# Paged latent attention in a two-layer decoder step: score rows by sequence, token block and head, and value pages of 32 partitions

## The reference

```python
q_lat = jnp.einsum('bthd,rhd->bthr', q_nope, w_uk)
s_past = (jnp.einsum('bthr,bsr->bhts', q_lat, ckv_past)
          + jnp.einsum('bthd,bsd->bhts', q_rope, kr_past))
s_new = (jnp.einsum('bthr,bsr->bhts', q_lat, ckv_new)
         + jnp.einsum('bthd,bsd->bhts', q_rope, kr_new))
sc = jnp.concatenate([s_past, s_new], axis=-1).astype(jnp.float32) * scale
pr = jax.nn.softmax(sc, axis=-1).astype(ckv_past.dtype)
o_lat = (jnp.einsum('bhts,bsr->bthr', pr[..., :npast], ckv_past)
         + jnp.einsum('bhts,bsr->bthr', pr[..., npast:], ckv_new))
o = jnp.einsum('bthr,rhd->bthd', o_lat, w_uv)
```

## Time and profile before

| what | value |
|---|---|
| runs of the kernel, median (lowest, highest) | 2039.2 us (2038.97, 2047.94) |
| time of the profiled execution | 2037.94 us |
| its span, first to last instruction | 2036.2 us |
| mean granted TensorE clock | 0.996 |
| PE busy | 2017.8 us, 99% of the span |
| DVE, ACT, POOL busy | 1045.8, 716.4, 279.1 us |
| DMA traffic | 322.44 MB |

### The profile page before, as it was taken

The page is one execution under the profiler, slowest core; times in us unless marked ns, Lnnn a source line. Parts: engine busy times, 40 slices in busy tenths (PEclk is TensorE's granted clock), DMA queues, the critical chain, the costliest instruction groups (busy, mean ns, idle before and its releaser), DMA issues.

```text
span 2036.2 us, 49885 instructions
## 1 busy us (share of the span) xinstructions
PE 2017.8 (99%) x21040; PEld 1915.6 (94%) x21040; DVE 1045.8 (51%) x1605; ACT 716.4 (35%) x1127; POOL 279.1 (14%) x520
## 2 busy tenths in 40 slices
PE   9999999999999999999999999999999999999998
PEld 9998888889999999999999988888999999999998
DVE  7876423366656444433367754234775654444333
ACT  5454114265333222222234531323653332222221
POOL 0003555600000000000000044565000000000000
PEclk9999999999999999999999999999999999999999
DMA  6427899942433333233353298999224333332332
GB/s 230 130 72 263 296 357 325 361 131 67 139 99 95 94 91 93 87 96 87 99 179 105 84 307 299 335 341 364 83 69 131 104 94 94 91 96 86 95 90 75
DMA packets 165557, 322.44 MB, mean 158 GB/s; under 512 B 24419, under 2 KB 104854, under 8 KB 164822
## 3 DMA queue, kind: packets, MB, share of 16 engines
q10 hardware_dynamic: 46944, 147.87, 23.5%
q1 hardware_dynamic: 93814, 100.04, 14.9%
q0 software_dynamic: 24576, 71.34, 10.1%
HBM read 307.08 MB, written 12.08 MB: 157 GB/s over the span
## 4 chain that ended last, share of the span: by engine, by line
PE 95%; DVE 2%; ACT 1%; DMA 1%; issue 0%; ACTq 0%; SPq 0%; DVEq 0%
PE PS L1921 28%; PE PS L1923 27%; PE PS L1922 27%; PE PS L2177 3%; PE PS L2207 3%; PE PS L1974 2%; PE PS L2182 1%; DMA vpg<-in_cache_vals 1%; PE PS L2233 0%; PE PS L2375 0%; PE PS L1960 0%; DVE wl L699 0%; PE PS L1981 0%; PE PS L2337 0%; DVE kxl L706 0%
## 5 line engine op out<-in xcount | busy, mean ns | idle before, releaser
L1921 PE MATMUL PS<-hh,wh 128*128 128x260 f32 x3008 | 862.6, 287 | 1.3 <-DVE gtmp L1104 1.0
L1923 PE MATMUL PS<-hl,wh 128*128 128x260 f32 x3008 | 850.6, 283 | 0.0
L1922 PE MATMUL PS<-hh,wl 128*128 128x260 f32 x3008 | 849.5, 282 | 0.0
L1921 PEld LDWEIGHTS PS<-hh,wh 128*128 128x128 f32 x3008 | 567.2, 189 | 14.9 <-issue 7.1
L1923 PEld LDWEIGHTS PS<-hl,wh 128*128 128x128 f32 x3008 | 567.4, 189 | 0.0
L1922 PEld LDWEIGHTS PS<-hh,wl 128*128 128x128 f32 x3008 | 567.0, 189 | 0.3
L699 DVE TENSOR_TENSOR wl<-raw,wh 128x1024 fp32r<-128x1024 f32 (+4 forms) x326 | 351.0, 1078 | 303.9 <-ACT wh L1455 302.9
L1455 ACT ACTIVATE wh<-raw 128x1024 fp32r<-128x1024 f32 (+4 forms) x326 | 304.3, 937 | 485.2 <-PE PS L1923 478.2
L1921 PE MATMUL PS<-fh,wh 128*128 128x260 f32 x704 | 199.3, 283 | 0.0
L1923 PE MATMUL PS<-fl,wh 128*128 128x260 f32 x704 | 198.7, 282 | 0.0
L1922 PE MATMUL PS<-fh,wl 128*128 128x260 f32 x704 | 198.6, 282 | 0.0
(11 more groups left out here) (362 smaller groups left out, 2989.5 us busy)
## 6 DMA issues: line engine op xcount, KB each, us to landing
raw<-in_wpack ACTq DMA_DIRECT2D x238, 512.0 KB, 3.6
vpg<-in_cache_vals SPq DMA_DIRECT2D x256, 128.0 KB, 6.1
vpg<-in_cache_vals POOLq DMA_DIRECT2D x256, 128.0 KB, 5.4
kpg<-in_cache_keys SPq DMA_DIRECT2D x224, 144.0 KB, 4.5
kpg<-in_cache_keys POOLq DMA_DIRECT2D x112, 144.0 KB, 4.8
ky<-in_cache_keys POOLq DMA_DIRECT2D x96, 144.0 KB, 4.1
raw<-in_wpack ACTq DMA_DIRECT2D x48, 256.0 KB, 2.9
raw<-in_wpack ACTq DMA_DIRECT2D x16, 384.0 KB, 3.1
```

The lines of the kernel that those rows point to most:

```text
L1921: pe.matmul(out, w[0], x[0], start=first, stop=False)
L1922: pe.matmul(out, w[1], x[0], start=False, stop=False)
L1923: return pe.matmul(out, w[0], x[1], start=False, stop=last)
```

## The change

- **Score rows.** The rows of a sequence are now 32*bj + 8*j + h, for the token block j (position modulo 4) and the head h; the two groups g of sequences lie in different columns of the bank. `scs` goes from 128x4096 to 128x2x1024.
- **Keys.** The host stores the positions of a key page in the order j, then i, with position 4*i + j. `keys(w)` makes 8 x 4 matmuls of 64 columns for the latent, whose stationary is a window that slides over `qlz` so that the query lies in columns 8*j to 8*j+7, and 4 matmuls of 64 columns for the rotary part with one block-diagonal stationary `qrz`. So 36 matmuls of 64 columns stand in place of 8 of 256 and 16 of 64. Where a unit lies in the split buffer (now units 1 and 7 alone), 9 matmuls of 32 columns on column group 3 follow the 36.
- **Banks.** There are 5 key banks of 4, 8, 8, 8 and 4 units in place of 8 of 4.
- **Softmax.** Maxima and sums are over blocks j too: `over_blocks` makes a reduce, a 32x32 transpose, a reduce, a copy and a transpose on DVE, each waiting for the one before. Exponentials come in 4 x 2 pieces of 128x256 and those of the new token in two pieces. PE turns 16 blocks in place of 32, two of the new token's probabilities in place of one, four of the result in place of two, and starts O with 4 matmuls of 512 and 4 of 256 columns.
- **Values.** A unit is now four pages of one sequence, each page in 32 partitions of 1024 floats (four positions to a partition). `values(c, g)` waits for four units and makes 16 matmuls of 256 columns with 8 columns of `pT` as stationary; the four units are released at its end.
- **Buffers.** Key slots for the long run go from 4 to 5 (slot 5 may be filled for the first time after the prompt's last attention product, "pe o7"), value slots from 11 to 13 (later from 9 to 11). Some tiles of the linear attention move, with waits for the values or stores that lay there.

```diff
-K_SLOTS, V_SLOTS = 3, 6
+K_SLOTS, V_SLOTS = 3, 9
+KEY_BANKS = ((0, 4), (4, 12), (12, 20), (20, 28), (28, 32))
-KEY_SLOT = [4, 3, 0, 1, 2, 4, 0, 3, 1, 2, 4, 3] + [0, 1, 2, 4] * 5
+KEY_SLOT = [4, 3, 0, 1, 2, 5, 4, 3, 0, 1, 2, 5] + [4, 0, 1, 2, 5] * 4
...
+                def over_blocks(src, op):
+                    dve.tensor_reduce(by_row[:, 0:2], src, AX.X, op).then_inc(*mark("dve_step"))
+                    dve.wait_ge(*own())
+                    dve.transpose(turned_rows[:, :], by_row[:, :]).then_inc(*mark("dve_step"))
+                    dve.wait_ge(*own())
+                    dve.tensor_reduce(best[:, :], turned_rows[:, :].rearrange("p (j h) -> p h j", j=4), AX.X, op).then_inc(*mark("dve_step"))
+                    dve.wait_ge(*own())
+                    dve.tensor_copy(spread[:, :, :], best[:, :].unsqueeze(1).broadcast_to([128, 4, 8])).then_inc(*mark("dve_step"))
+                    dve.wait_ge(*own())
+                    dve.transpose(by_row[:, :], spread[:, :, :].rearrange("p j h -> p (j h)")).then_inc(*mark("dve_step"))
+                    dve.wait_ge(*own())
...
                 def keys(w):
-                    for kk in range(2):
-                        for bj in range(4):
-                            for q, pages in key_pages(w, bj):
-                                ins = pe.matmul(out[32 * bj:32 * bj + 32, q, :], qlz[:, kk, 120 * g + 32 * bj:120 * g + 32 * bj + 32],
-                                                pages[:, :, PAGE * kk:PAGE * kk + PAGE], start=(g, kk) == (0, 0), stop=False)
-                    for t in range(4):
-                        for bj in range(4):
-                            for q, pages in key_pages(w, bj):
-                                ins = pe.matmul(out[32 * bj:32 * bj + 32, q, 32 * t:32 * t + 32], qlz[:, 2 + t, 120 * g + 32 * bj:120 * g + 32 * bj + 32],
-                                                pages[:, :, 2 * PAGE:KCOL], start=False, stop=(g, t) == (1, 3) and q.stop == 2)
+                    blocks = [(kk, j) for kk in range(2) for j in range(4)] + [(2, 0)]
+                    for part in range(2 if KEY_SLOT[w] == K_SLOTS else 1):
+                        for kk, j in blocks:
+                            for bj in range(4):
+                                for q, pages in key_pages(w, bj)[part:part + 1]:
+                                    stationary = latent_query(kk, 4 * g + bj, j) if kk < 2 else qrz[:, 4 * g + bj, :, :].rearrange("p j h -> p (j h)")
+                                    ins = pe.matmul(out[32 * bj:32 * bj + 32, q, :], stationary,
+                                                    pages[:, :, PAGE * kk + 32 * j:PAGE * kk + 32 * j + 32], start=(kk, j) == (0, 0), stop=kk == 2)
...
-                def values(col):
+                def values(c, g):
+                    pe.wait_ge(*upto(f"free pt{c // 2}n"))
+                    first = 8 * c + 4 * g
+                    for u in range(first, first + 4):
+                        pe.wait_ge(*upto(f"values {u}"))
+                    for j in range(4):
+                        for bj in range(4):
+                            u = first + bj
+                            ins = pe.matmul(bank("O")[32 * bj:32 * bj + 8, 256 * g:256 * g + 256],
+                                            pT[c // 2 % 2][:, 2 * g + c % 2, 32 * bj + 8 * j:32 * bj + 8 * j + 8],
+                                            vpg[VALUE_SLOT[u]][:, j, :], start=False, stop=(c, g, j) == (7, 1, 3))
+                            if j == 3 and u < 63:
+                                ins.then_inc(*mark("values_read", f"read V{u}"))
...
+                for c in range(8):
+                    for g in range(2):
+                        numbers = [page_numbers(mybir.EngineType.SP, 4 * c + 2 * i + g, 0) for i in range(2)]
+                        for bj in range(2):
+                            u = 8 * c + 4 * g + bj
+                            sp.wait_ge(*upto(SLOT_LEFT[VALUE_SLOT[u]] if VALUE_HOLDER[u] is None else f"read V{VALUE_HOLDER[u]}"))
+                            for page in range(4):
+                                sp.dma_start(vpg[VALUE_SLOT[u]][32 * page:32 * page + 32, :, :].rearrange("t j r -> t (j r)"),
+                                             a["cache_vals"][bass.ds(l, 1), bass.ds(numbers[page // 2][2 * (page % 2) + bj], 1), :, :].rearrange("a n (t j) r -> t (a n j r)", j=4)).then_inc(
+                                    *mark(f"values_loaded{VALUE_SLOT[u]}", f"values {u}" if page == 3 else None, 16))
```

More of the change, by code:

```diff
@@ L287, in plan @@
         lin(name)
-        groups.extend(f"K{w // 4}" for w in range(KEY_START[n], KEY_START[n + 1]) if w % 4 == 0)
+        groups.extend(f"K{k}" for k, (first, _) in enumerate(KEY_BANKS) if KEY_START[n] <= first < KEY_START[n + 1])
         if n == 1:
@@ L296, in plan @@
     for c in range(8):
-        if c < 7:
-            groups.append(f"pt{c + 1}n")
+        if c % 2 == 0 and c < 6:
+            groups.append(f"pt{c // 2 + 1}n")
         if c == 2:
@@ L1289, in head_variances @@
                 def head_variances(p):
+                    dve.wait_ge(*upto("out S1 1"))
                     for e in range(2):
@@ L2166, in keys @@
                 def keys(w):
-                    g, n = w % 2, w // 4
-                    if w % 4 == 0:
+                    g, n = w % 2, next(k for k, (_, last) in enumerate(KEY_BANKS) if w < last)
+                    first, last = KEY_BANKS[n]
+                    if w == first:
                         begin(f"K{n}")
-                    c = 256 * (w // 2 % 2)
-                    out = bank(f"K{n}")[:, c:c + 256].rearrange("p (a c) -> p a c", a=2)
+                    c = 32 * (last - first) * g + 64 * ((w - first) // 2)
@@ L2185, in keys @@
+                    if w < last - 1:
                         ins.then_inc(*mark("keys_read", f"read K{w}"))
@@ L2204, in values @@
+                def values(c, g):
+                    pe.wait_ge(*upto(f"free pt{c // 2}n"))
+                    first = 8 * c + 4 * g
+                    for u in range(first, first + 4):
                         pe.wait_ge(*upto(f"values {u}"))
+                    for j in range(4):
                         for bj in range(4):
-                            r = slice(32 * bj, 32 * bj + 32)
-                            ins = pe.matmul(bank("O")[r, 256 * g:256 * g + 256], pT[c % 2][:, col % 4, r],
-                                            vpg[VALUE_SLOT[u]][:, bj, :], start=False, stop=u == 63)
@@ L2399, in _ @@
                 for k in range(2):
-                    ins = turn(bank("Ot")[:, 128 * k:128 * k + 128], Oacc[:, 128 * k:128 * k + 128])
+                    for g in range(2):
+                        a = 2 * k + g
+                        ins = turn(bank("Ot")[:, 128 * a:128 * a + 128], Oacc[:, g, 128 * k:128 * k + 128])
                 ins.then_inc(*mark("group_ready", "pe Ot"))
```

272 lines of the change are left out of this document (144 added, 128 removed).

## The result

The changed kernel takes 2135.45 us (median of 4 runs, 2126.69 to 2140.67) against 2043.15 us for the kernel before on the same chip: ratio 1.0447, 95% interval 1.0400 to 1.0494. The profiled execution took 2140.67 us, its span is 2139.0. The forecast was 2066, with a range of 2020 to 2105. So it is slower, as forecast, but by 4.5% in place of 1.3%, and outside the range.

A forecast was written before the change was run, and what follows sets the result against it. PE and DMA were taken as bounds a few per cent apart. PE would save 10.0 us a layer, but value pages at 260 GB/s would end the value stages 13.3 and 15.3 us later: 2036.2 + 28.6 = 2064.8 span, 2066 us, range 2020 to 2105.

The forecast's parts named there:

- What bounds the kernel: Whole kernel: PE busy 99%; where the cache is read, PE and DMA are two bounds a few per cent apart.
- The loads: Value pages written to 32 partitions instead of 128 load slower; value stage ends 13.3 us later in layer 0, 15.3 in layer 1.
- I take 260: Value-page rate in GB/s assumed for 32-partition loads, between 231 from the store rows and 373 for dense 128-partition loads.
- the worst form of the conflict: The 32-partition store rows, 231 to 234 GB/s for a full DMA share, cited against the harder-limit rival.
- PE-bound case: Value pages at 373 GB/s, loads in time: PE gives its 10.0 and the 2.0 of wait, -22 in all, 2016 us.
- line for 285 GB/s: Forecast by rate of value pages: at 285 GB/s, the rate if the conflict met half the bytes, 2047 us.
- PE, keys: Key stage: nine sets of 64 columns take 1.0 us for 1.33 a unit; with split units, -8.6 us a layer.
- PE, the rest: Fewer transposes -2.3 us, added transposes and O's starting set +0.9 a layer; value matmuls unchanged.
- that rival (2186 us): Value stage: 8-column weights don't share the array, the four matmuls of a set run one after another, +85 us a layer; chance 0.02.
- DVE and ACT: Softmax chain between key and value stages: added operations use up 0.8 us of slack, leaving nothing to 0.3 us; taken as nothing.
- They limit harder: Rival: page loads below 231 GB/s, or PE's clock falls in its waits; 2097 to 2160 us, chance 0.10.
- The fast rival: The four quarters even out above 295 GB/s and the value stage is PE's again; 2016 to 2028 us, chance 0.20.

The follow-up runs named there:

- e3: The changed kernel with SP issuing a unit's four value pages in the order 0, 2, 1, 3 and POOL in 2, 0, 3, 1: 2124.76 us.
- e5: The changed kernel with each value page on every fourth partition instead of 32 adjacent ones, ACT permuting score columns to match: 2042.76 us.
- e9: As e5, but two pages of a unit interleave in partitions 0 to 63 and two in 64 to 127: 2113.16 us.
- e4: The kernel before, with each latent key matmul of 256 columns cut into four of 64, 48 matmuls a unit for 24: 2083.41 us.
- e7: As e1, but only the first 128 of a key page's 288 columns loaded and read, wrong scores, 36 matmuls kept: 2019.61 us.
- e1: The changed kernel with value pages loaded into 128 partitions as before, so the values are wrong: 2042.93 us.
- e6: As e1, but key units in the old form of 8 matmuls of 256 columns and 16 of 64, wrong scores: 2039.14 us.
- e8: As e5, but key units cut in two, 16 matmuls one linear step earlier and 20 at the old place: 2045.56 us.

## Why the prediction was wrong, step by step

**What bounds the kernel.** Right: both bounds lie close together, and a slower page load came out in PE at once.

**The loads: the step that failed.** The term "I take 260" was mis-sized. In layer 0 the first value load is issued at 289.6 us and the last page lands at 460.1. With the 18 us of weights, 33.6 MB / 152.5 us = 220 GB/s; in layer 1, 1343.5 to 1521.9, 33.6 / 160.4 = 209. The same stretches as windows, with all that the DMA moves in them:

```profile
289.60:460.10 170.50, 136.43 (x1561) 109.82 (x1550) 44.77 (x77) 43.40 (x75) 65.17 (x132) 0.93 1.03 254
1343.50:1521.90 178.40, 138.38 (x1527) 111.78 (x1516) 43.06 (x74) 41.45 (x72) 64.99 (x132) 0.89 1.03 242
```

For a share of 1 this is 247 and 235 GB/s, and 242 / 1.04 = 233 between 350 and 390 us, where hardly anything but value pages and weights is moved. The store gave 231 to 234. So the row that the prediction had as its lower bound, "the worst form of the conflict", was the rate itself, and the step that failed was to go above it because four pages go to four quarters and the conflict might be partial. It is not, or hardly: e3's other order gave 0.5%. The 209 and 220 are lower still because the sum has the weights at 373 GB/s, a rate that nothing reaches beside these pages, and leaves out the last key pages: the first window holds 43.3 MB, where value pages and slabs are 40.4. The start was 6.6 us later than the 283 assumed. With 289.6 and 220 GB/s the prediction's own sum gives 289.6 + 153 + 18 = 460.6 for the last page, as it must, since the 220 comes from there. What this tests is the step from the last pages to the end of the stage: 464 to 466 us, measured 466.2. The mechanism and the form of the sum held, its rate did not. The value pages' own part, changed against e5, is 2139.0 - 2040.3 = 98.7 us of span; the prediction had 2064.8 - 2014 = 51, against its own PE-bound case. (Its line for 285 GB/s is 2 us off: the sum as it stands gives 2045 and not 2047.)

The rule of the Trainium skill ("SBUF — State Buffer", "Door 1: The DMA port swizzle"), cited there with 218 GB/s for 8 ports and 2113 us, was the better estimate: 209 to 220 were measured, and 2135. It is no sharp limit, since e9, whose pages reach 8 ports each by the same table, moved 237 and 231 GB/s by the same sum.

**PE, keys: the second step that failed.** "64 columns pay no surcharge" is right for a unit (1.14 us where 1.1 was forecast, and 0.92 for 0.89 in e4) and wrong for the stage, because the supply of instructions had no term in the sum at all. -8.6 us a layer became +2.7 to +3.8 in e5, with 8.3 and 9.2 us of stops. e7, with the same matmuls and half the key bytes, has 121.7 and 122.1 us, 7.4 and 7.1 less than before: the term as forecast, with 1.3 us of stops left in it. So the 36 matmuls are worth what was said only while instructions arrive. (The split unit 7 took 1.57 us rather than the 2.0 assumed.) In the changed kernel the stops are 12.9 and 10.3 us, more than in e1 or e5: the longest, 4.16 us at 302.70, comes when value loads already run (from 289.6), and the longest of e1 is 2.5. In the same part of layer 0 e3 has one of 4.66 and e9 one of 4.44 us, e5 at most 1.97. So the conflict of the value loads seems to delay the instructions too. The 25 ns between starts of the Trainium skill's rule ("TensorE: Matmul & The Clock Gate", "Wait — 56ns, not 53.3ns?") played no part: 64 records, spread over four column groups, start in 0.92 us, 14.4 ns each, in e4. It would have given a slower key stage as well, but for a reason that these records refute.

**PE, the rest.** About right. With loads in time the value stage is 104.2 us for 109.2 and 106.6, 2.8 and 2.4 less beyond the wait of 2.2, and the piece between the stages is 0.5 us longer (11.0 for 10.5): -2.3 and -1.9, where -1.4 was summed. The calls keep their length (324.15 - 322.31 = 1.84 us to the next linear for 1.87), so 8-column weights share the array, and that rival (2186 us) is out. The set that starts O is 321.72 - 321.18 = 0.54 us for 0.445.

**DVE and ACT.** Right that it hides. DVE's timeline of the changed kernel, from the last maximum to the scale:

```profile
311.96 0.42 DVE L1061 TENSOR_REDUCE mxs<-scs 128x2 f32<-128x256 f32 x1 [15.69 <-ACT scs L1689]
...
313.31 0.21 DVE L1066 STREAM_TRANSPOSE turned_rows<-by_row 128x32 f32<-128x32 f32 x1
313.56 0.21 DVE L1068 TENSOR_REDUCE best<-turned_rows 128x8 f32<-128x32 f32 x1
313.80 0.18 DVE L1070 COPY spread<-best 128x32 f32<-128x32 f32 x1
314.02 0.21 DVE L1072 STREAM_TRANSPOSE by_row<-spread 128x32 f32<-128x32 f32 x1
314.27 0.17 DVE L1127 TENSOR_SCALAR nms<-by_row 128x2 f32<-128x2 f32 x1
```

The steps start about 0.24 us apart rather than 0.15, 2.5 us for 1.7, and PE turns the first scores 317.38 - 311.44 = 5.9 us behind its first matmul after the key stage, as before (308.32 - 302.38).

**The rivals.** "They limit harder" (2097 to 2160) is what came, with a chance of 0.10. Its picture was half right. The waits are 64.8 us in 24 calls, 2.7 us each, where it spoke of 2 us in each of 16 calls a layer, and the clock does fall in them: of the value stage of layer 0, 143.9 = 104.2 + 29.3 of waits + 10.4 of slower matmuls. But those 10.4 us should have cost little, since DMA stays at 1.04 while pages load and the last page sets the end; they would otherwise have been waits. No run tests this. The fast rival (2016 to 2028) needed two things, pages that don't conflict and instructions in time: e5 has the first alone and ties, e7 has both, with fewer key bytes, and takes 2019.6.

What is shown and what is not: that the stops are late instructions follows from their place, from the counts and the times of the packets, and from e4, e6, e7 and e8. Why a packet comes late is less sure: e7 says that it is the page loads beside it, and no run delays or speeds the packets alone. Not tried: key units of 16 pages with 128 columns to a matmul, which would halve the instructions at the same columns.

## What to carry to other kernels

When a page's layout is chosen for TensorE, the 32 partitions of each transfer are a choice of their own: spread over the whole memory (every fourth) they cost nothing here, adjacent they cost 3.9 to 4.5% of the kernel, every second one of a half 3.5%. Count the instructions of a burst as well as its columns: where page loads fill the DMA, 36 short matmuls in 1.1 us ran out of instructions, and 24 in 1.4 us did not. And where the nearest row of the trace gives a rate, here a store of 0.2 us, don't take a value above it without a reason that a run shows; then compare like with like, all bytes for a share of 1.

## What the runs showed of the hardware

- With value pages in 32 adjacent partitions the DMA moves 242 GB/s at a share of 1.04, with pages on every second partition of a half 287 at 1.04, and on every fourth partition 348 at 0.98 (350 to 390 us, weights included; up to 384 in 340 to 360), with rows of 4 KB in all three. With 4 KB rows the share per byte is a little lower than with 1 KB rows: 349 GB/s at 0.97, where e1 has 362 at 1.06 (360 to 380 us).
- Instructions are fetched over the DMA in packets of 16.4 KB, by our estimate 267 bytes for a float32 matmul with its weights (25 packets more in e4 for 1536 matmuls more). PE stopped 16 times inside key units of the changed kernel, for up to 4.2 us, with every semaphore met, when short matmuls and dense loads came together. Each stop ended 1.3 to 1.6 us after a packet of that queue.
- A stop or wait of 2 to 4 us often brings the clock to its lower level. In the two stages of layer 0 of the changed kernel there are ten such gaps over 2 us, and after eight of them the granted clock falls to 0.50, with matmuls of a linear 0.22 us apart for 0.12 and a value call of 3.4 us for 1.9; after the waits from 379.3 (3.40 us) and 437.3 (3.48 us) it does not.
- A change from linears to key matmuls and back costs 0.37 us beyond the columns (e8), of which 0.1 is in the first matmul of the linear behind it and 0.09 in the last one ahead.
